# One projection item in each of the first 34 attention slots, prompt attention in the 37 slots from the 35th

## The reference, cut to what matters

```python
def token_mixer(xn, conv_prev, attend, w_in, b_forget, conv_w, conv_b, w_up_conv, w_up_attn, w_mix_out):
    z = xn @ w_in
    cb, cc, cx, q, k, v, fz, g_conv, g_attn = split_combined(z)
    ...
    logf = jax.nn.log_sigmoid(fz.astype(jnp.float32) + b_forget.astype(jnp.float32))
    ...
def fox_prompt(q, k, v, logf):        # blocks of 128 queries, causal, 8 heads x 64
    ...
        sc = jnp.einsum('bqhd,bkhd->bhqk', qi, k, preferred_element_type=jnp.float32) * scale
        sc = sc + di[:, :, :, None] - dk[:, :, None, :]
        ...
        return jnp.einsum('bhqk,bkhd->bqhd', p.astype(v.dtype), v)
def fox_sample(q, k, v, logf, k_past, v_past, logf_past):
    sp = jnp.einsum('bqhd,bkhd->bhqk', q, k_past, preferred_element_type=jnp.float32) * scale
    sp = sp + d_new[:, :, :, None] + rev[:, :, None, :]
    ...
    out = (jnp.einsum('bhqk,bkhd->bqhd', p[..., :n_past].astype(v_past.dtype), v_past)
           + jnp.einsum('bhqk,bkhd->bqhd', p[..., n_past:].astype(v.dtype), v))
```

## Time and profile before

| what | us |
|---|---|
| median of three runs | 2031.48 |
| profiled execution | 2032.28 |
| its span | 2030.6 |
| PE busy in the span | 1877.7 |
| slots 0 to 9, from 70.8 to 149.2 | 78.5 |
| slots 10 to 27, to 268.2 | 119.0 |
| slots 28 to 63, to 507.2 | 239.0 |
| slots 64 to 73 and the reload, to the first convolution product at 547.8 | 40.6 |

### The profile page before, as it was taken

One profiled execution on the slowest core, in us unless ns is written; L12 is line 12 of the kernel. 1 busy time (PEld: TensorE's weight loads), 2 busy tenths in 40 slices (PEclk: granted clock), 3 DMA queues, 4 the chain that ended last, 5 costly groups with the idle time before them and its releaser, 6 DMA issues.

```text
span 2030.6 us, 33501 instructions
## 1 busy us (share of the span) xinstructions
PE 1877.7 (92%) x12402; PEld 1112.9 (55%) x12402; DVE 832.1 (41%) x1867; ACT 442.4 (22%) x1021; POOL 250.7 (12%) x381
## 2 busy tenths in 40 slices
PE   6999988888999999999999898995999999999994
PEld 4677655555588868888864467443333333333331
DVE  5644476777666423333354506335111111111115
ACT  3111133444301011111111205231222222212213
POOL 0203233233100000000000000000111111111120
PEclk9999999999999999999999999997999999999997
DMA  7759999999912130210111204444999999999966
GB/s 264 265 169 355 350 359 334 351 339 354 328 41 95 47 120 11 63 52 11 63 65 64 85 1 156 145 158 164 362 381 385 380 370 377 372 371 377 367 223 262
DMA packets 208162, 458.55 MB, mean 226 GB/s; under 512 B 18721, under 2 KB 47418, under 8 KB 207618
## 3 DMA queue, kind: packets, MB, share of 16 engines
q1 hardware_dynamic: 177554, 365.30, 50.3%
q0 software_dynamic: 30448, 91.13, 12.6%
HBM read 432.44 MB, written 32.17 MB: 229 GB/s over the span
## 4 chain that ended last, share of the span: by engine, by line
PE 81%; DVE 6%; DMA 4%; issue 3%; ACT 3%; DVEq 1%; SPq 1%; POOLq 0%; POOL 0%; ACTq 0%
PE ps L1322 17%; PE ps L1632 11%; PE ps L1663 6%; PE ps L1151 6%; PE ps L1387 6%; PE ps L1643 5%; PE ps L1416 5%; PE ps L1166 3%; PE ps L1672 3%; PE ps L1123 3%; PE ps L1505 2%; PE ps L1274 2%; PE ps L1254 2%; PE ps L1132 1%; DMA kraw<-in_cache_k 1%
## 5 line engine op out<-in xcount | busy, mean ns | idle before, releaser
L1632 PE MATMUL ps<-gu,xgT 128*64 128x512 f32 x1024 | 226.8, 595 | 0.9 <-ACT xgT L1983 0.9
L2166 DVE STREAM_TRANSPOSE kt<-kraw 128x1024 f32<-128x1024 f32 x128 | 151.1, 1218 | 28.5 <-DMA kraw<-in_cache_k 19.5
L1322 PE MATMUL ps<-xnT,ring 128*128 128x264 f32 x672 | 160.5, 390 | 1.3 <-DMA xnT<-xn_d 1.3
L861 POOL DMA_DIRECT2D vpage<-in_cache_v x228 | 122.4, 537 | 293.1 <-PE ps L1274 234.9
L2904 DVE TENSOR_TENSOR sig_a<-ps,sig_a 128x256 f32<-128x256 f32 x32 | 13.6, 424 | 324.6 <-ACT sig_a L1987 324.6
L1632 PEld LDWEIGHTS ps<-gu,xgT 128*64 128x64 f32 x1024 | 70.6, 137 | 131.9 <-issue 128.8
L1322 PEld LDWEIGHTS ps<-xnT,ring 128*128 128x128 f32 x672 | 128.5, 192 | 24.8 <-DMA xnT<-xn_d 2.2
L1663 PE MATMUL ps<-wd,hidT_a 128*64 128x512 f32 x512 | 118.6, 605 | 19.0 <-ACT hidT_a L1993 11.0
L1643 PE MATMUL ps<-gu,xgT 128*32 128x512 f32 x1024 | 115.8, 592 | 0.0
L1151 PE MATMUL ps<-xnT,early 128*128 128x352 f32 x320 | 101.3, 472 | 4.4 <-DVE xnT L2110 4.4
L1151 PEld LDWEIGHTS ps<-xnT,early 128*128 128x128 f32 x320 | 60.7, 194 | 38.2 <-issue 8.8
(11 more groups left out here) (446 smaller groups left out, 2931.6 us busy)
## 6 DMA issues: line engine op xcount, KB each, us to landing
kraw<-in_cache_k SPq DMA_DIRECT2D x256, 256.0 KB, 5.1
wd<-in_w_expert_down SPq DMA_DIRECT2D x31, 2048.0 KB, 21.2
gu<-in_w_expert_gate SPq DMA_DIRECT2D x30, 2048.0 KB, 20.3
gu<-in_w_expert_up SPq DMA_DIRECT2D x30, 2048.0 KB, 24.6
vpage<-in_cache_v POOLq DMA_DIRECT2D x228, 256.0 KB, 5.7
ring<-in_w_in SPq DMA_DIRECT2D x12, 1024.0 KB, 8.0
yy<-y_d SPq DMA_DIRECT2D x16, 512.0 KB, 9.9
early<-in_w_in SPq DMA_DIRECT2D x6, 1024.0 KB, 11.5
```

Of the source, the lines that this page charges most:

```text
L861: eng.dma_start(vpage[value_place(n)][:, p, :], t["cache_v"][ds(page, 1)].rearrange("a s d -> (a s) d")).then_inc(v_in[value_place(n)], 16)
L1322: last = nc.tensor.matmul(bank(R.bank(name, f, q))[:, 0:QT], weight[:, k], src[:, k, cols], start=k == 0, stop=k == HK - 1)
L1632: last = nc.tensor.matmul(bank(0)[h * BA:(h + 1) * BA, :].rearrange("p (x n) -> p x n", x=2), src[:, k, 0:BA], weight[:, k, :, h * DE // 2 ...
L2166: nc.vector.transpose(kt[n % 2].rearrange("p c e s -> p (c e s)")[:, x * 1024:(x + 1) * 1024], kraw[n % 2].rearrange("p c d -> p (c d)")[: ...
```

## The change

`items(n)` gives one item to every slot 0 to 33. The order of the items is changed in one place: the sample tile of the second half of v (`("v", 1, PT)`) comes after five items of the first half instead of after nine, so that it is there when slot 17 weighs the first sequence's new tokens. Prompt attention starts six slots later, in slot 35, and has 37 slots instead of 43, so it ends in the same slot 71. The stores of k shift from slots 30 to 38 to slots 36 to 44, the new tokens' scores from slot 5 to slot 6, and the loads of weights and decays in SP's loop shift with their readers.

```diff
         REST = [(f, n) for f in range(KC) for n in range(COLS - 1)]
         VTILES = [PT] + list(range(PT))
-        ITEMS = ([("q", f, n) for f, n in REST] + [("v", half, i) for half in range(2) for i in VTILES]
+        ITEMS = ([("q", f, n) for f, n in REST] + [("v", 0, i) for i in VTILES[:5]] + [("v", 1, PT)]
+                 + [("v", 0, i) for i in VTILES[5:]] + [("v", 1, i) for i in VTILES[1:]]
                  + [("k", f, n) for f, n in REST])
-        PROMPT0, PROMPT_SLOTS, KOUT0 = 29, 43, 30
+        PROMPT0, PROMPT_SLOTS, KOUT0 = 35, 37, 36
 
         def items(n):
 
-            first = n + min((n + 1) // 2, 6)
-            return ITEMS[first:first + (2 if n < 12 and n % 2 == 0 else 1)]
+            return ITEMS[n:n + 1]
...
-            if n == 5:
+            if n == 6:
                 R.add("dve", "snew", banks=TURNS)
                 R.add("dve", "lf", banks=(0, 1, 4))
...
-                if n == 7:
+                if n == 8:
                     R.made(sp, "q", 1, 1)
                     early_load(0, O_V)
-                if n == 9:
+                if n == 12:
                     R.made(sp, "q", 3, 1)
                     early_load(1, O_V)
-                if n == 15:
+                if n == 22:
                     R.made(sp, "v", 0, PT - 1)
                     early_load(0, O_K)
-                if n == 24:
+                if n == 31:
                     R.made(sp, "v", 1, PT - 1)
                     early_load(1, O_K)
-                if n == 28:
+                if n == 34:
                     R.made(sp, "k", 1, 1)
                     sp.wait_ge(neg_stored, 16)
                     load_negk(0)
-                if n == 35:
+                if n == 40:
                     R.made(sp, "k", 3, 1)
                     sp.wait_ge(xn_stored, 16)
                     load_negk(1)
```

## The result

The changed kernel takes 2046.0 us, the median of seven runs (2042.3 to 2055.6), against 2031.5 in the same comparison; the ratio is 1.0068 (interval 1.0048 to 1.0088). The forecast was 2027 with a range up to 2041: wrong in sign and outside the range. I take the loss as 12 us.

A forecast was written before the change was run, and what follows sets the result against it. The PE bounds the loop to slot 27; in slots 28 to 63 PE, DVE, ACT and DMA wait for each other. Terms 13.5 + 3.1 - 25.2 + 3.7 = -4.9 us gave 2027, range 2011 to 2041.

The forecast's parts named there:

- Slots 0 to 33, +3.1 us of new waits: Item slots before the prompt section: 2.1 us wait in slot 1 plus 1.0 us for v slots.
- 13.5: Fixed work of six more item slots and one more new-values product, moved ahead of the prompt section: 13.5 us.
- part (d): Slots 0 to 33: reloads of `early` have their waits fulfilled long before SP comes to them; nothing counted.
- part (a): Slot 1: its scores wait for bank 5, which ACT empties after the forget gates' logarithm; 2.1 us.
- part (c): Slots 10 to 25, v items: demand of 380 GB/s at DMA's edge, 1.0 us taken between bounds 0 and 6.3.
- Rival C: Some load comes late for its new slot (k weights before slot 30), a few us; near 2031, chance 0.04.
- Slots 34 to 63, 213.8 us: Prompt section: 210.8 us from slot prices plus 3.0 for remaining DMA waits; against 239.0 before, minus 25.2.
- the bursts of slots 33 and 35: Double slots of 11.23 and 14.11 us, left out of the price; some 6 us less with the slow clock behind.
- B: Slower: without single slots DVE and ACT cannot catch up, double slots cost 8.65 us or more; 2052, chance 0.15.
- A: DMA sets the whole pace, bytes from slot 10 on take 358 us again; 2019, chance 0.29.
- The rest, +3.7: Slots 64 to 73 and input reload: two more halves, 4.4 us, less 0.7 for a less full DMA queue.
- What is gained or lost can only be idle time and clock: Whole kernel: the PE's products keep their sum, and fixed work and halves only change place.

The follow-up runs named there:

- all loads apart: Changed kernel with ACT copying slot 0's scores first, decays asked for sooner, v and k weights later, `negk` halves two slots apart: 2036.0 us, ratio 0.9999.
- the changed kernel without values: Changed kernel without loading the values of units 2 to 53, products running on old data: 2040.3 us, ratio to before 1.0035.
- half the dose: Kernel before with two items only in slots 0, 2 and 4, prompt attention in 40 slots from slot 32: 2043.6 us, ratio 1.0046.
- seven and eight pairs: Kernel before with two-item slots 0 to 12 (seven) or 0 to 14 (eight), prompt attention from slot 28 or 27: 2048.0 and 2045.8 us.
- The kernel before with its own decays apart: Kernel before with the two `negk` halves of later head pairs loaded two slots apart: 2032.2 us, ratio 0.9985 (0.9970 to 1.0001).

## Why the prediction was wrong

- **Slots 0 to 33, +3.1 us of new waits: this step failed.** Measured is +27.2 for the part where I had 13.5 + 3.1 = 16.6. The PE waits there for 8.5 us (mean of 10.9, 6.9, 9.1, 8.4, 7.4), and 4.1 us are lost to the low clock; the other 14.6 are the fixed work, which I had 1 us too small. What failed in it is part (d), "I count nothing" for the moved loads.
- Its part (a), the wait in slot 1, was right in cause and size (2.24 for 2.1) but I left out the slow item behind it, 1.6 us.
- Its part (c), v slots at the edge of DMA for 1.0 us: the rate was not the trouble. The kernel with all loads apart moves the same bytes in 95.6 us, at 368 GB/s and with 1.2 us of PE waits for values; my figure was 94.7. The changed kernel takes 100.4 to 103.3. The Trainium skill ("DMA: Bandwidth & Descriptors", "Where 436 GB/s comes from") has a limit near 358 GB/s for this. My estimate by it, 5.7 us in place of 1.0, would have come nearer to the number, but the measured 368 is above that limit, so it is not what made the wait.
- Its part (d) was where the cause lay. I asked whether the moved loads come in time for **their own** readers, and they do, but for a wait of 1.3 to 1.5 us for weights in slot 30 in two of the profiles. I did not ask what stands **behind them** in SP's queue. Two loads side by side, 1.5 MB, set the next keys back, and the PE waits 3.1 to 5.4 us for these. Slot 22 is shown by experiment: with the two set apart the wait is gone. Rival C was near it, a late load of "a few us" with a chance of 0.04; I had the wrong load in it.
- **Slots 34 to 63, 213.8 us:** 219.4 measured (215.7 to 222.3). The direction held, the size didn't. Double slots cost 8.17 us in the mean (forecast 8.06), single ones 5.01 (4.39), slot 34 4.6 (2.8): 2.4 + 4.4 + 1.8 us more, less the 3.0 that I had added for DMA, are the 5.6 us. (Of the "four bursts or their echoes of 10 to 11 us" in my price there were three: slots 43, 49 and 51.) The waits for values went (7.5 us in the mean of four profiles of before, 0.1 in five of the changed kernel). But I let the bursts of slots 33 and 35 go with nothing in their place. The PE's waits to slot 62 stay 31.5 where they were 32.9. The late keys, once of slot 35, are now those of slot 48, and slots 34 and 35 have waits for `masked` and `ftop`, 1.8 and up to 2.0 us. With loads apart the section is 215.5.
- **The rivals.** B wants double slots at 8.65 us and more; they are at 8.17, and at 7.98 with all loads apart, so it is wrong, though the time came out on its side. A is wrong too: it keeps 358 us for slots 10 to 63, and they take 373 to 385 in the changed kernel and 368.3 with all loads apart.
- **The rest, +3.7:** +3.5.
- **"What is gained or lost can only be idle time and clock"** was right, but the sum priced only idle time. More than half of the loss is low clock. Why the changed kernel without values, half the dose, and seven and eight pairs lose 7 to 10 us more to it than the kernel before is shown only in part: the last three have waits of 2 to 7 us with low clock behind them, and 2 to 11 us more of it in the loop than the mean of before, with one profile each; the first has no more in the loop than that mean. The kernel with all loads apart still loses 2 us more than before, which eats its net gain. That stays open.

So against the kernel before as it stands the move itself is worth nothing that can be measured. The edits of the kernel with all loads apart took back 8 to 10 us by the medians, 12 to 14 by the ratios to the kernel before; in the loop 3.5 us of this is its start, and some 11 are loads that stood too close together. Two of these (decays and weights at slot 22) were brought together by the change; the halves of `negk` stood together before as well. The kernel before with its own decays apart is still 4 us ahead by the median (2032.2), which these runs can't tell from nothing.

## What to carry to other kernels

When a change moves a load, look at what is issued on the same queue next to it, and who waits for the transfer behind it; its own reader is the lesser question. Where DMA is near full, keep big side loads apart, by a unit of the stream or more here. Look for slow products behind a wait of the PE and price them with it (here a wait of 2.24 us cost 3.9 in slots 0 and 1, and one of 5.44 cost 8.0 in slots 22 and 23), and compare low-clock and net time apart, over many runs, before a cause is sought in one profile.

## What had not been expected of the hardware

- DMA can run for 95.6 us at 368 GB/s beside a PE that is busy for 94.3 of them, more than the 356 of the earlier trace rows.
- The time of DVE's own waits for keys says little: 48.6 us in the loop of the changed kernel, and 53.9 in the one with all loads apart, which is 8 to 10 us faster. Only the wait that the PE feels counts.

```profile
DVE kt L2166 <- DMA kraw<-in_cache_k: 48.6, 17, 13.6
```

```profile
DVE kt L2169 <- DMA kraw<-in_cache_k: 53.9, 21, 8.3
```

- Low stretches far behind the loop, in unchanged code, come in some executions of both kernels and not in others. The four between 680 and 825 us last 3.4 us each and lose 6.8 us together; over all profiles 30 to 42 us are lost behind the loop.
